# Attention's value product turned round, with the row sums divided inside TensorE

## The reference

```python
HEAD_DIM, Q_BLOCK, WINDOW = 64, 128, 128
def block_attention(q, k, v, sink):      # per block of 128 queries
    s = jnp.einsum("bqhgd,bkhd->bhgqk", qi, k) * scale
    p = softmax(concatenate([s, sink]))[..., :-1] if sink is not None else softmax(s)
    return jnp.einsum("bhgqk,bkhd->bqhgd", p, v)
...
y_a = o_attn.reshape(b, s, ATTN_Q) @ lp["w_attn_out"]
y_w = o_win.reshape(b, s, WIN_Q) @ lp["w_win_out"]
merged = gates[:, :, 0] * y_f + gates[:, :, 1] * y_c + gates[:, :, 2] * y_a + gates[:, :, 3] * y_w
```

## Time and profile before

| | us |
|---|---|
| median of 3 runs | 5593.83 (5588.25 to 5594.8) |
| the profiled execution | 5605.9 |
| its span, first to last instruction | 5604.1 |
| TensorE busy in the span | 4472.4 (80%) |
| VectorE busy | 3694.6 (66%) |
| ScalarE busy | 887.5 (16%) |
| POOL busy | 1583.3 (28%) |
| mean granted TensorE clock | 0.906 of full speed |

### The profile page before, as it was taken

One profiled execution on the slowest core, in us unless ns is written; L12 is line 12 of the kernel. 1 busy time (PEld: TensorE's weight loads), 2 busy tenths in 40 slices (PEclk: granted clock), 3 DMA queues, 4 the chain that ended last, 5 costly groups with the idle time before them and its releaser, 6 DMA issues.

```text
span 5604.1 us, 47094 instructions
## 1 busy us (share of the span) xinstructions
PE 4472.4 (80%) x14736; PEld 2601.9 (46%) x14736; DVE 3694.6 (66%) x8129; ACT 887.5 (16%) x2536; POOL 1583.3 (28%) x1310
## 2 busy tenths in 40 slices
PE   6999996889797666666689999978887876666665
PEld 4866785444443222222258567754444432222222
DVE  1745316688687888876608453177886878888765
ACT  1023201111211111111111332101111111111111
POOL 0000000334334454455400000013443345444552
PEclk9999998999899888888899999989998998888887
DMA  6100142899989999999761002339998999999996
GB/s 267 45 31 1 63 150 110 328 377 369 358 353 358 421 422 421 421 420 422 330 240 38 31 1 79 139 125 361 376 378 347 351 373 421 422 421 421 419 422 282
DMA packets 226377, 1585.28 MB, mean 283 GB/s; under 512 B 26064, under 2 KB 28368, under 8 KB 46672
## 3 DMA queue, kind: packets, MB, share of 16 engines
q0 software_dynamic: 184320, 1342.26, 59.2%
q1 hardware_dynamic: 41808, 240.02, 11.3%
HBM read 1579.03 MB, written 3.15 MB: 282 GB/s over the span
## 4 chain that ended last, share of the span: by engine, by line
PE 40%; DMA 33%; DVE 17%; issue 3%; DVEq 3%; ACT 2%; POOL 1%; SPq 0%; POOLq 0%; ACTq 0%
DMA B<-tables,R 18%; PE ps L478 8%; DMA A<-tables,R 6%; PE ps L488 5%; PE ps L619 5%; DMA H<-tables,R 4%; DVE A L1469 4%; DVE B L1437 3%; DMA B<-ws 3%; PE ps L604 2%; PE ps L495 2%; PE ps L508 2%; PE ps L724 2%; DMA R<-tables,R 2%; DVE A L1437 2%
## 5 line engine op out<-in xcount | busy, mean ns | idle before, releaser
L478 PE MATMUL ps<-B,A 128*128 128x512 f32 x2048 | 1179.5, 723 | 555.1 <-ACT A L893 555.0
L446 POOL DMA_INDIRECT B<-tables,R x716 | 866.0, 1209 | 1860.2 <-PE ps L478 814.9
L1437 DVE SCALAR_TENSOR_TENSOR B<-B,M 128x1024 f32<-128x1024 f32 x716 | 866.8, 1224 | 290.3 <-DMA B<-tables,R 262.9
L478 PEld LDWEIGHTS ps<-B,A 128*128 128x128 f32 x2048 | 448.5, 229 | 1209.4 <-ACT A L893 677.1
L478 PE MATMUL ps<-A 128*128 128x512 f32 x992 | 530.6, 670 | 155.2 <-ACT A L893 155.1
L488 PE MATMUL ps<-H,B 128*128 128x384 f32 (+1 forms) x2048 | 595.0, 445 | 66.6 <-DMA B<-ws 44.0
L446 POOL DMA_INDIRECT A<-tables,R x356 | 440.0, 1236 | 582.5 <-PE ps L478 370.6
L488 PEld LDWEIGHTS ps<-H,B 128*128 128x128 f32 x2048 | 399.7, 196 | 264.5 <-issue 56.2
L1437 DVE SCALAR_TENSOR_TENSOR A<-A,M 128x1024 f32<-128x1024 f32 x356 | 433.5, 1225 | 128.7 <-DMA A<-tables,R 116.2
L887 ACT ACTIVATE T<-T 128x2 f32<-128x2 f32 (+1 forms) x448 | 91.6, 205 | 2351.3 <-DVEq L1439 2351.1
L478 PEld LDWEIGHTS ps<-A 128*128 128x128 f32 x992 | 208.0, 217 | 442.3 <-issue 230.9
(11 more groups left out here) (206 smaller groups left out, 5052.3 us busy)
## 6 DMA issues: line engine op xcount, KB each, us to landing
B<-ws SPq DMA_DIRECT2D x120, 1024.0 KB, 6.8
B<-ws SPq DMA_DIRECT2D x128, 768.0 KB, 7.9
B<-tables,R POOLq DMA_INDIRECT x716, 18.4
A<-tables,R POOLq DMA_INDIRECT x356, 14.8
R<-tabs SPq DMA_DIRECT2D x2, 2176.0 KB, 12.3
H<-tables,R POOLq DMA_INDIRECT x192, 16.9
x<-xin SPq DMA_DIRECT2D x1, 2560.0 KB, 9.3
y<-M SPq DMA_DIRECT2D x1, 2560.0 KB, 7.9
```

The lines of the kernel that those rows point to most:

```text
L446: pool.indirect_dma_start(out=ring[s], out_offset=None, in_=tables[:, :], in_offset=bass.IndirectOffsetOnAxis(ap=EI[:, n:n + 1], axis=0),) ...
L478: mm = pe.matmul(ps[:, bk + c, :], diag[PE_AT[n] % DIAGS], v_row[:, c * 512:(c + 1) * 512], start=(n % SLOTS == 0), stop=(PE_AT[n] + 1 == ...
L1437: v.scalar_tensor_tensor(out=u_row, in0=u_row, scalar=1.0, in1=h2[:, g.tile, :], op0=ALU.mult, op1=ALU.mult, accum_out=dots[:, o:o + 1])
```

## The change

The blocks of probabilities are no longer transposed. Instead each block, as stationary operand, is multiplied with a diagonal matrix that holds the reciprocals of the 128 row sums (`scaler`, two buffers). That gives the transposed block already divided. VectorE makes the diagonal from the identity in a new function `inverse`, which stands ahead of the next unit's maximum, and signals it by `a_dg`, for which TensorE waits before the products.

The value product is turned round. The values (64 columns) are the stationary operand, and the transposed probabilities of two heads side by side (256 columns) the moving one. Two such products, `odd` = 0 and 1, write partitions 0 to 63 and 64 to 127 of a bank, so four heads that share their values make one group, and a group's result already has channels on the partitions: it needs no transposition and goes by one copy of ScalarE (`outputs`) into `BRc`. `PT` keeps a whole group, one buffer for windowed and one for full groups. The units are taken in groups of four, windowed and full in turn (`ORDER`). TensorE runs three groups' value products after the fifth, ninth and thirteenth place of a tile, and the fourth group's after the query transpositions of the next tile. `keep_running` is six products for the first two tiles and two for the others, and writes bank 6 instead of 7. The transpositions of `QO`, `QO` itself and VectorE's `out` are gone.

```diff
-        PT = [M[:, 1280 + i * 640:1280 + (i + 1) * 640] for i in range(2)]
-        MK = M[:, 2560:3584]
-        QO = M[:, 3584:4608]
+        PT = [A[:, 0:2560].rearrange("p (i c n) -> p i c n", i=5, c=4), M[:, 1280:3328].rearrange("p (i c n) -> p i c n", i=4, c=4)]
+        scaler = [M[:, 3328 + i * P:3328 + (i + 1) * P] for i in range(2)]
+        MK = M[:, 3584:4608]
...
+                def values(n, t, g):
+                    u, at = ORDER[4 * g], 4 * n + g
+                    pt, nb, c = PT[windowed(u)], blocks(t, u), (u % HEADS) // GROUP * HD + windowed(u) * P
+                    pe.wait_ge(a_pa.sem, a_pa.at(l, n * UNITS + 4 * g + 4))
+                    pe.wait_ge(a_pd.sem, a_pd.at(l, n * UNITS + 4 * g + 4))
+                    pe.wait_ge(a_on.sem, a_on.at(l, at - 1))
+                    for i in range(nb):
+                        block = 0 if t is None else (1, 2, 3, 4, 6)[i] if not windowed(u) else t + i if i < 3 else 6
+                        for odd in range(2):
+                            last = pe.matmul(ps[odd * HD:odd * HD + HD, 6 + g % 2, 0:2 * P], V[:, block, c:c + HD],
+                                             pt[:, i, 2 * odd:2 * odd + 2, :], start=(i == 0), stop=(i == nb - 1))
+                    last.then_inc(a_o.sem, 1)
...
-                    keep_running(6)
+                    if n:
+                        values(n - 1, t - 1 if t else None, 3)
+                    keep_running(n, 6 if n < 2 else 2)
...
+                    def transposes(p):
+                        u = ORDER[p]
                         split = dve_blocks(t, u)
+                        pe.wait_ge(a_dg.sem, a_dg.at(l, u0 + p + 1))
+                        pe.wait_ge(a_pa.sem, a_pa.at(l, u0 + p))
+                        pe.wait_ge(a_pd.sem, a_pd.at(l, u0 + p))
+                        for i in range(blocks(t, u)):
+                            bank, o = (4, i) if i < split else (5, i - split)
+                            last = pe.matmul(ps[:, bank, o * P:(o + 1) * P], Pb[p % 2][:, i * P:(i + 1) * P], scaler[p % 2],
+                                             start=True, stop=True)
+                        last.then_inc(a_t.sem, 1)
+
+                    for p in range(UNITS + 1):
+                        if p < UNITS:
+                            scores(p)
+                        if p:
+                            transposes(p - 1)
+                        if p in (5, 9, 13):
+                            values(n, t, p // 4 - 1)
...
-                pe.wait_ge(ot_ev.sem, ot_ev.at(l, TILES))
+                pe.wait_ge(a_on.sem, a_on.at(l, 4 * TILES))
...
+                def outputs(n, g):
+                    u, o = ORDER[4 * g], PLACE[n]
+                    j = (u % HEADS) // 2
+                    act.wait_ge(a_o.sem, a_o.at(l, 4 * n + g + 1))
+                    act.copy(BRc[CHUNK[n]][:, 3 if windowed(u) else 2, j:j + 2, o:o + P],
+                             ps[:, 6 + g % 2, 0:2 * P].rearrange("p (j n) -> p j n", n=P)).then_inc(a_on.sem, 1)
...
+                    def inverse(p):
+                        u, e = ORDER[p], p % 2
+                        v.wait_ge(a_exp.sem, a_exp.at(l, u0 + p + 1))
+                        total = sm[:, 2, e:e + 1]
                         if windowed(u):
+                            v.tensor_tensor(out=sm[:, 5, e:e + 1], in0=total, in1=sm[:, 3, e:e + 1], op=ALU.add)
+                            total = sm[:, 5, e:e + 1]
                             v.drain()
+                        v.reciprocal(sm[:, 4, e:e + 1], total)
                         v.drain()
+                        v.tensor_scalar(out=scaler[e], in0=ident, scalar1=sm[:, 4, e:e + 1], scalar2=None, op0=ALU.mult)\
+                            .then_inc(a_dg.sem, 1)
...
+                    for p in range(UNITS + 1):
+                        if p:
+                            inverse(p - 1)
+                        if p < UNITS:
+                            maxima(p)
+                        if p:
+                            pt_copy(p - 1)
...
+ORDER = [0, 1, 2, 3, 8, 9, 10, 11, 4, 5, 6, 7, 12, 13, 14, 15]
+SIDE = [p % 2 * 2 + p % 4 // 2 for p in range(UNITS)]
```

More of the change, by code:

```diff
@@ L664, in _, with keep_running @@
                 last.then_inc(kt_ps.sem, 1)
[L666 removed]
+                def keep_running(n, times):
+                    pe.wait_ge(a_on.sem, a_on.at(l, 4 * n - 1))
                     for i in range(times):
[L669 to L671 removed]
+                        pe.matmul(ps[:, 6, 0:384], ident, hTc[1][:, i % KD, :], start=True, stop=True)
+                keep_running(0, 10)
                 pe.wait_ge(kt_ev.sem, kt_ev.at(l, 1))
+                def values(n, t, g):
[10 more added lines that the diff above has]
+                    last.then_inc(a_o.sem, 1)
                 def attention(n, t):
@@ L705, in scores @@
                         last.then_inc(a_s.sem, 1)
-                    def transpose_part(u, i):
+                    def transposes(p):
+                        u = ORDER[p]
                         split = dve_blocks(t, u)
[L710 to L761, removed]
+                        pe.wait_ge(a_dg.sem, a_dg.at(l, u0 + p + 1))
@@ L1104, in _ @@
             v.sem_inc(a_pd.sem, 1)
-            v.sem_inc(a_on.sem, 2)
             v.sem_inc(mg_ev.sem, 2)
@@ L1286, in pt_copy @@
                         v.drain()
-                    def out(u):
-                        v.wait_ge(a_o.sem, a_o.at(l, u0 + u + 1))
-                        v.tensor_scalar(out=QO[:, u * HD:(u + 1) * HD], in0=ps[:, 6 + u % 2, 0:HD],
-                                        scalar1=sm[:, 4, u % 2:u % 2 + 1], scalar2=None, op0=ALU.mult).then_inc(a_on.sem, 1)
-                    for u in range(UNITS + 2):
-                        if u < UNITS:
-                            maxima(u)
-                        else:
-                            v.drain()
-                        if 1 <= u <= UNITS:
-                            pt_copy(u - 1)
-                        if u >= 2:
-                            out(u - 2)
+                        v.tensor_scalar(out=scaler[e], in0=ident, scalar1=sm[:, 4, e:e + 1], scalar2=None, op0=ALU.mult)\
+                            .then_inc(a_dg.sem, 1)
@@ new lines, in pt_copy @@
+                    def pt_copy(p):
+                        u = ORDER[p]
+                        split = dve_blocks(t, u)
+                        v.wait_ge(a_t.sem, a_t.at(l, u0 + p + 1))
+                        if p % 4 == 0 and n * 4 + p // 4 >= 2:
+                            v.wait_ge(a_o.sem, a_o.at(l, n * 4 + p // 4 - 1))
+                        v.tensor_copy(PT[windowed(u)][:, 0:split, SIDE[p], :],
+                                      ps[:, 4, 0:split * P].rearrange("p (i n) -> p i n", n=P)).then_inc(a_pd.sem, 1)
```

72 lines of the change are left out of this document (30 added, 42 removed).

## The result

The change makes the kernel slower: 5678.7 us (5662.4 to 5683.5, 4 runs) against 5594.3 us (5588.3 to 5596.0, 4 runs), a ratio of 1.0148 with a 95% interval of 1.0126 to 1.0169. That is 84 us. The forecast was 5630, +36, with a range up to 5668. The direction was right, the size was not.

A forecast was written before the change was run, and what follows sets the result against it. TensorE was taken to set attention's pace, so added time there lengthens the whole. Tiles and end summed to 281.7 us a layer against 263.9, two layers +36, giving a median of 5630 from 5593.8, range 5592 to 5668.

The forecast's parts named there:

- The clock: Rival, attention's second tile: gaps in the context tile bring full clock back later; some 25 us a layer, 5680; chance 0.05.
- Sum at full clock: Attention stage of one layer, all tiles and end added: 281.7 us against 263.9 before, +17.8.
- Context tile: Attention's first tile, heads of one block: the chain rules, 38.0 us.
- Second tile: Attention's second tile: twelve filler instructions kept, small burst ahead, 2.3 us for starting at half clock; 62.4 us.
- Third and fourth tile: Latent tiles of attention, from one query transposition to the next: 59.2 us each, +1.9 over before.
- Transposition becomes product: Attention's probability blocks: 0.225 us a block, two instructions; 0.90 us a windowed head, 1.125 a full one.
- Switching: Around each burst of value products on TensorE: 0.15 us on each side, 0.30 a burst, 12 us in all.
- Value product turned round: Attention's value product: paired instructions of 256 columns at 0.1055 us; 1.69 us a windowed group, 2.11 a full one.
- The new chain: Row sum, reciprocal and diagonal before TensorE's product: 2.79 us windowed, 2.57 full, from the maximum's start.
- No pairing: Rival, value product: 64-partition halves don't run side by side, 0.21 us an instruction, 65 us in all, 5695; chance 0.09.
- The diagonal is never late: Rival, chain before the product: half a microsecond shorter, so waits go, 28 us in all, 5602; chance 0.17.
- A block for the price of a transposition: Rival, diagonal product: a block takes 0.11 to 0.13 us and the chain is shorter, 5581 to 5562; chance 0.09.

The follow-up runs named there:

- fill6: The changed kernel with six filler products instead of two at the start of the third to fifth tiles; 5692.6 us, 1.0168.
- movefill: The changed kernel with the two filler products of the third to fifth tiles moved into the first diagonal's wait, and two added there in the first two tiles; 5636.7 us.
- identprod: The changed kernel with blocks multiplied by the identity, waiting for the exponent alone, division by the row sums left out; 5601.7 us, 1.0011.
- before_fill2: The kernel before the change with two filler products instead of six for the third to fifth tiles; 5585.6 us, 0.9972.
- identtrans: identprod with blocks transposed again instead of multiplied with the identity, division still left out; 5557.9 us, 0.9926.
- latediv: The changed kernel with blocks transposed again, waiting for the exponent alone, and the division done last, after the turned value product; 5628.0 us, 1.0053.
- latediv2: latediv with ScalarE's copy of the reciprocals and VectorE's multiplication taken ahead of the unit's exponent and maximum; 5580.6 us, 0.9974.
- before_wait: before_fill2 with four short VectorE operations between maximum and exponent in each latent tile's first unit, lengthening TensorE's wait; 5832.2 us, 1.0441.
- identtrans_wait: identtrans with the same four VectorE operations as before_wait; 5628.9 us in one execution.

## Why the prediction was wrong, point by point

The step that failed is the clock. The prediction carried full speed over to every latent tile and kept a later return of the clock only as the rival "The clock", at 0.05, for the second tile alone and started by the gaps of the context tile. It had worked out the wait that does the harm, as a number (4.79 us from the first scores to the first product where 4.03 were), and priced it at its own length. The wait itself was as forecast (1.17 us, 4.82 from the first scores to the first product); what was put at nothing is the clock behind it, some 52 us in the two layers. That is an estimate from the changed kernel's own tiles. At full clock one takes 60 us: the second layer's fifth, which has no fall, takes 63.6 with 3.7 of end, and the four without a fall in fill6 62.5 to 62.8 with 2.6 more of filler. With 62 for the second tile (65.2 in the second layer, less some 3 for its fall of 7) a layer would be 38.5 + 62 + 60 + 60 + 63.6 = 284, two layers 568, and 620.2 were measured. The remaining 38 us over the kernel before (530.3) are the price at full clock, against 36 forecast.

The rival "The clock" had 5680 for its price, and 5678.7 was measured. That is chance: it came from one whole tile a layer at half clock behind the gaps of the context tile, and the runs show shorter falls in almost every latent tile, each behind its own wait. In the changed kernel the context tile's stretch at half clock is 30.7 us instead of 23.9, and the clock is back before the second tile's scores.

The other terms:

- *Sum at full clock.* Forecast 281.7 us a layer, 284 by the estimate above. movefill measures 281.2 and 280.2 (5636.7 in all, 5630 forecast), but that flatters the forecast: two filler products stand in the wait there and not ahead of the scores, which makes each of six tiles some 1.2 us shorter than the change would be at full clock.
- *Context tile.* Forecast 38.0; 38.5 in both layers. With the chain off the path 32.7 (identprod).
- *Second tile.* Forecast 62.4; 63.2 and 62.2 in movefill, with two more filler products in the wait.
- *Third and fourth tile.* Forecast 59.2; 60 at full clock as above, 58.8 and 58.5 in movefill.
- *End.* Forecast 3.7; the fifth tile with the end takes 62.2 in movefill, 3.7 above the tile ahead of it.
- *Transposition becomes product.* Taken at 0.1125 us an instruction, 0.126 measured in the unit shown above (0.123 in the one with five blocks at 479.55, 1.38 us for ten): a little dearer. From one unit's products to the next scores it is 1.09 us windowed (491.22 to 492.31) and 1.32 in a full one (474.26 to 475.58), where 0.99 and 1.215 were taken: 0.1 a head too low, 1.6 us a tile. The tile came out only 0.8 above the forecast, bursts being cheaper among other things. From identprod to identtrans it is 6.8 us a tile at full clock, where the block prices give 8.
- *Switching.* Forecast 0.30 a burst. The burst of 20 instructions takes 2.31 us (482.60 to 484.91), 0.2 above the 2.11 for the instructions alone. That makes 8 us for the 40 bursts, not 12.
- *Value product turned round.* Right: 0.105. From before_fill2 (54.8) to identtrans (50.7 without a fall) a tile gets 4.1 us shorter; the output transpositions and VectorE's `out` went with it, so it isn't the value product's alone. The page "TensorE: Matmul & The Clock Gate" of the Trainium skill says in Part 3 that small products, placed on different tiles of the array, run concurrently in it. The trace agrees for halves of 64 columns: 0.105 us an instruction, against the 0.22 worked out for one alone from the earlier trace rows.
- *The new chain.* Right: 2.83 for 2.79, waits of 0.51 and 1.20 for 0.6 and 1.3. VectorE's scaling took 0.29 where 0.24 was taken.
- *Fillers.* Right as a price (57.3 to 54.8), and no sure protection of the clock where they stood.

Of the rivals, "No pairing", "The diagonal is never late" and "A block for the price of a transposition" are out by the rows above.

What remains open: the last unit of each tile has a wait of the same length (1.20 us) ahead of its product, and no fall began there in the changed kernel, while in latediv and latediv2 short falls did. Half of the latent tiles of fill6 and a quarter of those of before_wait were spared although each had the wait. So the wait makes a fall likely, not certain, and the runs don't tell what decides in a single case. The 12 us that the kernel came out shorter outside the stage say nothing of the change: over the profiled executions of all the versions here what lies outside the two stages takes between 5054 and 5080 us.

## What to carry to other kernels

When a change puts a step ahead of TensorE's work, price the idle time that it opens twice: by its length, and by what the clock does after it. Here 1.2 us of idle time, once a tile, was followed by falls that cost up to 10 us each (the fourth tile of the first layer, 70.3 against 60), and two filler products in the gap kept them away (movefill), while the same two ahead of the scores didn't. A division that can wait belongs behind the product, off the path: with it at the end the turned value product came out ahead, 0.9952 against 0.9972 for the kernel before with less filler. The two intervals overlap a little, but in the stage, in one profiled execution of each, it is 14 us.

## What the hardware showed unexpectedly

One added idle wait of TensorE at a tile's start, 1.30 us instead of 0.38, was followed in six of eight tiles by a granted clock of 0.50 (1.2 GHz) for 85 to 92 us, while TensorE was busy 79 of 80 us (before_wait). In the version with bursts of 256 columns the same wait was followed by 17 to 20 us at 0.50 (identtrans_wait), in the changed kernel by 3 to 24.
